# Two up-projections of a transformer kernel: seven block products in place of eight

## The reference

```python
y = mixer(...) @ w_out                       # token mixer, then output projection 1024 x 1024
x = x + gt1 * rmsnorm(y, g_post)             # residual
h = modulate(rmsnorm(x, g_pre_ffn), sh2, sc2)

def conv_ffn(h, p):                          # D_FF = 2816 = 22 * 128
    u = dwconv(h @ p['w_up'], p['ffn_conv']) + p['ffn_conv_b']   # w_up 1024 x 5632, 3 taps over tokens
    val, gate = jnp.split(u, 2, axis=-1)
    return (val * jax.nn.silu(gate)) @ p['w_down']               # w_down 2816 x 1024
```

## Time and profile before

| | |
|---|---|
| median of 3 runs | 3636.86 us (3633.42, 3636.86, 3645.36) |
| span of the profiled execution | 3639.3 us |
| TensorE matmul busy | 3469.9 us, 95% |
| TensorE weight loads busy | 3187.7 us, 88% |
| VectorE busy | 2010.0 us, 55% |
| ScalarE busy | 1552.9 us, 43% |
| POOL busy | 140.0 us, 4% |

### The profile page before, as it was taken

How to read it: one execution, slowest core, us unless ns; L and a number is a source line. 1 busy time by engine, 2 the same in 40 slices (tenths; PEclk the granted TensorE clock), 3 DMA queues, 4 the chain that set the end, 5 groups by cost and what they waited for, 6 DMA issues and landing times.

```text
span 3639.3 us, 71215 instructions
## 1 busy us (share of the span) xinstructions
PE 3469.9 (95%) x30719; PEld 3187.7 (88%) x30719; DVE 2010.0 (55%) x3131; ACT 1552.9 (43%) x2539; POOL 140.0 (4%) x267
## 2 busy tenths in 40 slices
PE   7999899999889979999999999999999999999999
PEld 4787779888877878888888999899999899999999
DVE  5477767787757745543335785232224653333676
ACT  4556654444337734433334654111114443333554
POOL 2000000000000001000000111000001000000000
PEclk9999999999989989999999999999999999999999
DMA  6233443223233124211113665111114421111665
GB/s 243 75 129 130 147 171 104 90 82 115 76 70 71 26 80 133 89 58 47 47 47 121 209 215 161 30 33 44 47 47 125 131 71 47 47 47 54 200 214 165
DMA packets 321840, 367.30 MB, mean 101 GB/s; under 512 B 14803, under 2 KB 261046, under 8 KB 321528
## 3 DMA queue, kind: packets, MB, share of 16 engines
q1 hardware_dynamic: 304424, 309.64, 27.3%
q0 software_dynamic: 17104, 53.11, 4.4%
HBM read 302.79 MB, written 59.90 MB: 100 GB/s over the span
## 4 chain that ended last, share of the span: by engine, by line
PE 57%; DVE 3%; ACT 2%; issue 1%; DVEq 0%; DMA 0%; POOL 0%; ACTq 0%
PE psum L3376 10%; PE psum L3378 10%; PE psum L3377 10%; PE psum L2351 4%; PE psum L2826 4%; PE psum L2827 4%; PE psum L2828 4%; PE psum L2353 4%; PE psum L2352 4%; PE psum L2688 1%; DVE u_val L3576 1%; DVE w_lo L3277 1%; PE psum L3323 1%; ACT u_val L3467 0%; DVE g L3581 0%
## 5 line engine op out<-in xcount | busy, mean ns | idle before, releaser
L3376 PE MATMUL psum<-mix_h_hi,w_hi 128*128 128x342 f32 (+5 forms) x1848 | 636.3, 344 | 17.1 <-DVE w_lo L3277 15.2
L3377 PE MATMUL psum<-mix_h_hi,w_lo 128*128 128x342 f32 (+5 forms) x1848 | 632.3, 342 | 0.0
L3378 PE MATMUL psum<-mix_h_lo,w_hi 128*128 128x342 f32 (+5 forms) x1848 | 631.9, 342 | 0.0
L2218 DVE TENSOR_TENSOR w_lo<-w_raw,w_hi 128x1024 fp32r<-128x1024 f32 (+1 forms) x167 | 195.9, 1173 | 398.4 <-ACT w_hi L2208 396.9
L3376 PEld LDWEIGHTS psum<-mix_h_hi,w_hi 128*128 128x128 f32 x1848 | 349.0, 189 | 47.5 <-DVE w_lo L3277 18.6
L2208 ACT ACTIVATE w_hi<-w_raw 128x1024 fp32r<-128x1024 f32 (+1 forms) x167 | 170.3, 1020 | 491.3 <-PE psum L2828 325.3
L3378 PEld LDWEIGHTS psum<-mix_h_lo,w_hi 128*128 128x128 f32 x1848 | 348.9, 189 | 26.8
L3377 PEld LDWEIGHTS psum<-mix_h_hi,w_lo 128*128 128x128 f32 x1848 | 349.2, 189 | 26.3
L3453 ACT ACTIVATE xs<-psum 128x1024 f32<-128x1024 f32 (+1 forms) x66 | 67.9, 1029 | 486.2 <-PE psum L3378 486.2
L2351 PE MATMUL psum<-down_ghi,w_hi 128*128 128x256 f32 x944 | 269.8, 286 | 0.6 <-DVE down_glo L2223 0.3
L2353 PE MATMUL psum<-down_glo,w_hi 128*128 128x256 f32 x944 | 266.9, 283 | 0.0
(11 more groups left out here) (490 smaller groups left out, 7999.1 us busy)
## 6 DMA issues: line engine op xcount, KB each, us to landing
w_raw<-in_w_down SPq DMA_DIRECT2D x118, 512.0 KB, 4.1
w_raw<-in_w_up SPq DMA_DIRECT2D x110, 512.0 KB, 3.7
w_raw<-in_w_in SPq DMA_DIRECT2D x59, 512.0 KB, 4.0
down_w_raw<-in_w_down SPq DMA_DIRECT2D x58, 512.0 KB, 3.9
rw_operands<-step_set SPq DMA_DIRECT2D x16, 1024.0 KB, 6.3
mod_w<-in_w_mod POOLq DMA_DIRECT2D x32, 512.0 KB, 6.1
w_raw<-in_w_out SPq DMA_DIRECT2D x32, 512.0 KB, 3.6
unit<-rw_operands SPq DMA_DIRECT2D x22, 512.0 KB, 5.0
```

The lines of the kernel that those rows point to most:

```text
L3376: nc.tensor.matmul(out, k.w_hi[:, s, w], xh[:, kk, x], start=(kk == 0), stop=False)
L3377: nc.tensor.matmul(out, k.w_lo[:, s, w], xh[:, kk, x], start=False, stop=False)
L3378: last = nc.tensor.matmul(out, k.w_hi[:, s, w], xl[:, kk, x], start=False, stop=(kk == KD - 1))
```

## The change

The up-projection of a pair of tiles (val i, gate i) is read as a product of 2 x 2 blocks: weights by (val, gate) and by the lower and upper 512 input features, h by the same feature halves and by the two token halves. The eight block products and four sums become seven products P1 to P7 with sums before and after (the Winograd form of Strassen's method):

- the moving operands t1 = h11 - h12, t2 = h22 + t1, t3 = h12 - h22, t4 = h21 - t2 (with the halves' low parts added) are made once per block (`add_turns`), and rounded into high and low parts (`round_turns`, `low_turns`);
- per pair VectorE makes four sums of weight blocks of 512 columns (`add_weights`, and one in `weight_low`), and the results are combined as they come out of PSUM (`take`, five operations per pair);
- P1 and P2 of val tiles 0 to 7 (they need only half 0) are made early, beside the chain of half 1, for the 11 half jobs; the later steps of a pair are P6 P7 P5 P4 P3 for those eight pairs and P1 P6 P7 P5 P2 P4 P3 for the other 14;
- a step is now half a weight tile (4 blocks of 128 by 512 weight columns) on one token half: 12 matmuls of 512 columns, in the second block 24 of 258. Four raw weight tiles and four split half tiles are kept, and weights are prepared three steps ahead in place of one;
- token halves are 512 and 512, and 516 and 516;
- the gated rows go to DRAM as they are made (`g_dram`), and the down-projection reads them back by parts of 256 tokens: part 0 row by row, parts 1 to 3 as one load of 22 rows each on POOL's queue, part p+2 issued at the end of part p, ahead of the x rows.

The core of the diff:

```diff
-MIX_PARTS = (448, 576)
+MIX_PARTS = (512, 512)
...
+def plan_steps(banks):
+    steps = [("O", u, h) for u in range(2 * KD) for h in range(2)]
+    if banks == 1:
+        early = [("P1", EARLY[0])]
+        for last, i in zip(EARLY, EARLY[1:]):
+            early += [("P1", i), ("P2", last)]
+        early.append(("P2", EARLY[-1]))
+    else:
+        early = [(kind, i) for i in EARLY for kind in ("P1", "P2")]
+    late = [(kind, i) for i in range(KF)
+            for kind in (("P6", "P7", "P5", "P4", "P3") if i in EARLY else ("P1", "P6", "P7", "P5", "P2", "P4", "P3"))]
+    return steps + early + late
...
+    def weight_low(dve, s):
+        src, r = source(s)
+        dve.wait_ge(*w_high.at(s + 1))
+        nc.vector.tensor_tensor(ring[s % 4][:, 1, :], src, ring[s % 4][:, 0, :].bitcast(F32), ALU.subtract).then_inc(w_low.sem, 1)
+        if s + 1 < STEPS and s + 1 >= first_late:
+            kind, i = steps[s + 1]
+            if kind == "P6":
+                add_weights(dve, i)
+            elif kind == "P4":
+                v = raw[tile_val(i) % 4]
+                dve.drain()
+                nc.vector.tensor_tensor(tmp[1][:, :], v[:, 512:1024], tmp[1][:, :], ALU.add).then_inc(w_added.sem, 1)
+
+    def add_weights(dve, i):
...
+        dve.drain()
+        nc.vector.tensor_tensor(tmp[0][:, :], g[:, 0:512], g[:, 512:1024], ALU.add).then_inc(w_added.sem, 1)
+        dve.drain()
+        nc.vector.tensor_tensor(g[:, 0:512], g[:, 0:512], v[:, 0:512], ALU.add).then_inc(w_added.sem, 1)
+        nc.vector.tensor_tensor(tmp[1][:, :], tmp[0][:, :], v[:, 0:512], ALU.add).then_inc(w_added.sem, 1)
...
+        def bank_free(s):
...
+            elif kind == "P6":
...
+                if i >= SETS:
+                    pe.wait_ge(*took.at(5 * (i - SETS) + 1))
...
+            elif kind == "P4":
+                pe.wait_ge(*took.at(5 * i + 2))
+            elif kind == "P3":
+                pe.wait_ge(*took.at(5 * i + 3))
...
+        def centre_val(i):
+            act.wait_ge(*took.at(5 * i + 5))
+            act.wait_ge(*c11_kept.at(KEPT[i] + 1))
+            if i:
+                act.wait_ge(*g_stored.at(16 * i))
+            nc.scalar.activation(uv[:, :], xv(i)[:, left + 1:left + 1 + SEQ], ACT.Identity,
...
+        def add_turns(kk):
...
+            dve.drain()
+            tt(f["t1"], h0[0][kk][:, :].bitcast(F32), b12, ALU.subtract)
+            tt(f["t3"], b12, b22_row, ALU.subtract)
+            dve.drain()
+            tt(f["t1"], f["t1"], h0[1][kk][:, :].bitcast(F32), ALU.add)
+            dve.drain()
+            tt(f["t2"], b22_row, f["t1"], ALU.add).then_inc(t_added.sem, 1)
+            dve.drain()
+            tt(f["t4"], h0[0][kk + 4][:, :].bitcast(F32), f["t2"], ALU.subtract)
+            dve.drain()
+            tt(f["t4"], f["t4"], h0[1][kk + 4][:, :].bitcast(F32), ALU.add).then_inc(t4_added.sem, 1)
...
+        def take(s):
...
+            dve.wait_ge(*acc_done.at(s + 1))
...
+            dve.drain()
+            if kind == "P6":
...
+                last = tt(part, late_out(i, 1), half12, ALU.subtract)
+            elif kind == "P7":
+                last = tt(half22, part, late_out(i, 2), ALU.add)
+            elif kind == "P5":
+                last = tt(half22, half22, late_out(i, 3), ALU.subtract)
+            elif kind == "P4":
+                last = tt(half21, part, late_out(i, 2), ALU.add)
+            else:
+                last = tt(half12, late_out(i, 3), part, ALU.subtract)
+            last.then_inc(took.sem, 1)
...
+        for s in range(STEPS):
+            kind, i = steps[s][0:2]
+            at = s - late_at[i] if s >= first_late else None
...
+            if at == 1 and i:
+                val_tap(i - 1, 2)
+            elif at == 2 and i:
+                product(i - 1)
+            if s + 3 < STEPS:
+                weight_low(dve, s + 3)
...
+            if at == 0 and i:
+                val_tap(i - 1, 0)
+            elif kind == "P3":
+                gate_taps(i)
...
+            if s in (first_late, first_late + 1):
+                low_turns(TURNS[3 + s - first_late])
+            if s >= first_late:
+                take(s)
...
+    def load_part(self, pool, p):
+        pool.dma_start(self.g_part[p % 2][:, :, :],
+                       self.k.g_dram[:, :, self.cols(p)].rearrange("n p c -> p n c")).then_inc(self.part_landed[p], 16)
...
         for p in range(SEQ // PART):
             pool.wait_ge(self.low, KF * (p + 1))
+            if p + 2 < SEQ // PART:
+                self.load_part(pool, p + 2)
             for kk in range(4):
                 self.load_x(pool, p, kk)
```

More of the change, by code:

```diff
@@ L2183, in nth @@
     def nth(self, i):
-        return i // 3 + 1 if i < self.TWO else self.TWO // 3 + (i - self.TWO) // 2 + 1
+        return sum(self.slot(j) == self.slot(i) for j in range(i + 1))
     def depth(self, i):
@@ L2917, in vector @@
             elif i + 2 == self.total:
-                self.next.weight_low(dve, 0)
+                for s in range(2):
+                    self.next.weight_low(dve, s)
             if q == 7:
@@ L3206, in vector @@
             self.finish_rows(dve, self.last, half)
-FIRST = 11
+EARLY = list(range(8))
+QUEUE = len(EARLY)
+KEPT = {i: j for j, i in enumerate(EARLY + [i for i in range(KF) if i not in EARLY])}
+X_BUFFER = [i if i < 8 else 6 + i % 2 for i in range(KF)]
+FIRST_ROWS = 8
 def half_groups(n):
@@ new lines, in spreads, with chain @@
+            pe.wait_ge(*diags.at(norm(a, second)))
+            for t, m in half_groups(n):
+                if t == 0:
+                    last = nc.tensor.matmul(spread_out[:, 0:4 * P], k.ones[:, :], dg[:, 0:4, :], start=True, stop=True)
+                elif m < P:
+                    last = nc.tensor.matmul(spread_out[:, t * P:t * P + m], k.ones[0:m, :], dg[0:m, t, 0:m],
+                                            start=True, stop=True)
+            last.then_inc(spread.sem, 1)
+        def chain(a, e, kk):
+            if e == 1 and kk == 1:
+                sums(a)
+            elif e == 2 and kk == 3:
+                spreads(a, 0)
+            elif e == 5 and kk in (0, 2):
+                sum_residual(a, kk // 2)
+            elif 6 <= e <= 10 and kk == 1:
+                sum_residual(a, e - 4)
+            elif e == 10 and kk == 3:
+                sum_residual(a, 7)
+            elif e == 12 and kk == 2:
+                spreads(a, 1)
@@ L3507, in scale_tile @@
[L3507 to L3520 removed]
+            dve.drain().then_inc(diags.sem, 1)
@@ new lines, in scale_rows @@
+        def scale_rows(a, j0):
+            dve.wait_ge(*spread.at(norm(a, 1)))
+            dve.wait_ge(*x_stored[a].at(16 * KD))
+            dve.drain()
+            for j in range(j0, j0 + 4):
+                row = y[a][:, order[a][j], :]
+                if shift is not None:
+                    nc.vector.tensor_tensor(row, row, spread_out[:, 0:n], ALU.mult).then_inc(scaled.sem, 1)
+                else:
+                    nc.vector.scalar_tensor_tensor(out=row, in0=row, scalar=gain_pre(order[a][j]), in1=spread_out[:, 0:n],
+                                                   op0=ALU.mult, op1=ALU.mult).then_inc(scaled.sem, 1)
@@ new lines, in tap, with gate_taps @@
+        def tap(i, gate, q):
+            u, x = (ug, xg) if gate else (uv, xv(i))
+            dve.drain()
+            return nc.vector.scalar_tensor_tensor(out=u[:, :], in0=x[:, left + q:left + q + SEQ],
+                                                  scalar=rows_of(k, f"{conv}{q}", i + side[0 if gate else 1]),
+                                                  in1=u[:, :], op0=ALU.mult, op1=ALU.add)
+        def gate_taps(i):
+            dve.wait_ge(*centred_g.at(i + 1))
+            tap(i, True, 0)
+            tap(i, True, 2).then_inc(tapped_g.sem, 1)
```

903 lines of the change are left out of this document (541 added, 362 removed).

## The result

The changed kernel takes 3760.06 us, the median of 4 runs (3755.24 to 3766.93), beside 3639.71 us before (3633.42 to 3645.36): a ratio of 1.033, 95% interval 1.031 to 1.0351. It is 120 us slower; 3616 had been forecast, and 3668 was the upper end.

The account below looks back on a forecast made before the run. TensorE, busy 95% of the span, was taken to bound the kernel. Up stages -19 and -11 us, stage ends +1 and DRAM blocks +8 made -21, set on the median: 3616 us, range 3572 to 3668.

Parts of the forecast that it names:

- the hand-over: Each up-projection pair: VectorE waits twice for ScalarE's centring, 1.34 us with a 0.61 us low part in front, up to 0.85 each.
- Late pairs: Up-projection: VectorE's 19.4 us cycle just fits TensorE's 19.53; 0.4 and 0.2 us lost a pair, 5.6 and 2.8 per mixer.
- Early pairs: The eight early pairs turn VectorE-bound: cycle 17.8 us against TensorE's 13.95, costing 27 and 26 us in the two mixers.
- rival 4: Early pairs: recurring waits keep the clock low; all 60 matmuls at 1.2 GHz give +126 us, 3742; chance 4%.
- Rival 2: VectorE bounds every pair, its cycle 1.5 us above the count (19.0 early, 20.9 late): 3663 us; chance 20%.
- Rival 1: VectorE overlaps better: early pairs run at 16.5 us and the turn costs 20 us: 3577 us; chance 20%.
- Streaming: Up-projection matmuls, seven products for eight: 429.8 and 438.3 us, gaining 62 and 60 us in the two mixers.
- The turn: Before P6 of pair 0 TensorE idles 20 us, then 6.5 more; with slow clock 31 and 30 us in the mixers.
- The second wait: In the turn, TensorE waits 6.5 us more until P7 is taken.
- The blocks by way of DRAM: Down stages: loads of parts 1 to 3 delay the x rows, 0 to 8 us for each of six, 8 in all.
- the 14 us that I had worked out by it: If queues take fair turns, the weights lose up to 2.4 us beside each block, some 14 for the six.
- The wait for the last gated row: End of the up stage: the wait of 3 to 4 us gets 1 longer, +1 for both mixers.

Follow-up runs that it names:

- Experiment 1: ScalarE's two centrings of a pair moved behind the next weight block's high part, against the changed kernel: 3638.63 us.
- kernels 5 and 8: 5: changed kernel with centrings behind the next high part, P4's own bank, sum kept: 3613.88 us; 8: also gated rows two at a time, SP's queue: 3607.68 us.
- experiments 8 and 9: On kernel 5: gated rows of parts 1 to 3 two at a time on SP's queue, 3607.68 us; parts 2 and 3 fetching one row, 3612.24 us.
- experiment 7: Four weight sums per pair made by POOL in place of VectorE, against kernel 5 with the turn's sums batched (3613.38 us): 3758.19 us.

## Why the prediction was wrong

- **The step that failed: "Twice a pair it also waits for ScalarE to centre a row ... with a step's low part of 0.61 in front, so up to 0.85 each".** That is the hand-over if the low part can run beside the centring. I took it from the earlier trace rows, where it can, and checked VectorE's order only. ScalarE's order has the centring ahead of the next high part, so the low part was behind the centring too: 1.83 us twice and 0.70 once, 4.36 us a late pair for 1.7 forecast. Experiment 1 moves that order alone and gives back 121 us, and 0.78 at the tap.
- **Late pairs.** "19.4" for VectorE's cycle measured 22.50: excess over TensorE 3.0 us in the first mixer and about 2.6 in the second, x14 = 42 and 36 us for 5.6 and 2.8. I had written that 19.4 under 19.5 leaves no room for a late hand-over, and then took 0.4 and 0.2 a pair, near the lower bound of 0 to 1.5.
- **Early pairs.** 17.8 us measured 20.7 to 22.9: from pair 0's P4 to pair 7's it is 155.3 us, so seven pairs at 8.2 over 13.95 are 58 us for 27. Part is the same fault, part rival 4 in a weaker form: P4 alone, not all five steps, runs at half clock, and since VectorE waits for P4 (2.41 us) its slow clock isn't covered, as I had assumed it was. Together with the late pairs this makes (42 - 5.6) + (58 - 27) = 67 us for the first mixer; the stage was 63 over the forecast.
- **The rivals.** Rival 2, VectorE bounds every pair, was the case, with 20% of the chance. Its sign was right and its place nearly: the centring behind a taken product, but VectorE waited at the next low part and not at the tap. Its price was half or less: +1.5 us a pair, where it was 3.1 late and 4.7 early. (Its term for the second mixer's late pairs should read 0.78 by its own figures, 20.9 less 19.92 and 0.2, not 0.88.) Rival 1 did not come true even in kernels 5 and 8: an early pair takes 17.4 us there, not 16.5, and the first wait of the turn is 23.7 us, not shorter. Their 3614 and 3608 lie near the 3616 of the forecast in part by luck: kernel 5's up stages take 500 and 509 us for the 509 and 511 forecast, while the stretches behind them are 11 and 10 longer than before, where 9 in all had been taken.
- **Streaming** was right: 12 matmuls a step at 0.2326, and 0.1196 for the estimated 0.1186 at 258 columns, some 4 us in the second mixer. The gain of nearly 122 us in streaming exists; it was turned into waits.
- **The turn.** 20 us for the first wait measured 23.77 and 22.6, ended by ScalarE's keeping of the last early P2, which is queued behind the roundings of t2, t3 and t1, not by VectorE's low part, which was ready 1.1 us earlier. The second wait was 3.5 for 6.5. In sum 27 for 26.5: right in size, with another engine at the end of the first wait than the one named.
- **The blocks by way of DRAM.** 8 us were taken, with 0 and 48 as bounds. The stretches behind the up stages grew by 10 and 11. Of these, experiments 8 and 9 put 4 to 5 on the blocks; no wait of TensorE ends at the x rows, as forecast, but the weights were late, which was forecast only beside the Trainium skill's rule. The Trainium skill ("DMA: Bandwidth & Descriptors", on queues and arbitration) has queues served by turns; the 14 us that I had worked out by it was above what was measured, and the trace agrees with it as to who is hurt (the weights, at 367 GB/s and a share of 0.98). The wait for the last gated row grew by 1.8 and 1.5 us (5.10 and 4.94 for 3.29 and 3.42), for 1 in all.

## What to carry to other kernels

When an engine comes within a few per cent of being the bound, write down the queues of both engines of each hand-over, not one: a queue worked off in order that waits for A before it makes B turns every consumer of B into a consumer of A. A wait belongs behind the work that others need and that is ready, and moving four lines was worth as much here as the arithmetic saved. What a wait costs is read from what comes last behind it: POOL's 11 us wait in experiment 7 isn't what its sums hang on in the late pairs. A saving of an eighth of TensorE's work left a margin of 0.13 us a pair; the forecast should then have gone to the slower case until each hand-over had been traced through both queues.

## What the runs showed that was not expected

- A wait of 6.23 us on TensorE made the next twelve matmuls of 512 columns take 0.427 us for 0.2326 (granted clock 0.85 in the 100 us around it): 2.5 us on top, and a new wait on the engine that reads the result.
- POOL stood idle at the drain between two of its sums: 1.0 to 1.5 us in most early pairs, where one DMA issue stands ahead of the sums, 3.15 in most late ones with two, and 8.1 and 7.2 where the second of them fetches 1024 KB. Why wasn't tested.
- DMA engines reached 367 GB/s at a busy share of 0.98 with a 2816 KB load and the x rows together, and the weights, for which quiet windows of that stage move some 187 GB/s, were then late.
- Executions of kernels that are equal ahead of the change reach the output projection at 1303.8 to 1317.0 us, so a difference of a few us is read from there on, not from the span.
